# A two-layer diffusion backbone: bias among the first unit's matmuls, two modulation pieces moved, two more PSUM banks, new early order

## The reference

```
x += 0.5*g * swiglu(modulate(rms_norm(x)))        # half step, d_ff 2816
x +=     g * mixer(modulate(rms_norm(x))) @ w_out # attention A | windowed attention B | bidirectional SSD
x += 0.5*g * swiglu(modulate(rms_norm(x)))
```

## Time and profile before

| | us |
|---|---|
| median of 3 runs | 1890.67 |
| runs | 1890.6 to 1891.48 |
| the profiled execution | 1888.78 |
| its span, first to last instruction | 1887.1 |
| PE busy | 1811.9 (96%) |
| DVE busy | 1423.3 (75%) |
| ACT busy | 752.0 (40%) |
| mean granted TensorE clock | 0.968 of 2.4 GHz |

### The profile page before, as it was taken

How to read it: one execution, slowest core, us unless ns; L and a number is a source line. 1 busy time by engine, 2 the same in 40 slices (tenths; PEclk the granted TensorE clock), 3 DMA queues, 4 the chain that set the end, 5 groups by cost and what they waited for, 6 DMA issues and landing times.

```text
span 1887.1 us, 26111 instructions
## 1 busy us (share of the span) xinstructions
PE 1811.9 (96%) x9314; PEld 1496.1 (79%) x9314; DVE 1423.3 (75%) x2351; ACT 752.0 (40%) x1147; POOL 51.6 (3%) x101
## 2 busy tenths in 40 slices
PE   8999999997999899899999999999999799899999
PEld 5788888886776577688888888888888578589999
DVE  5887877788877767887777678777786888756665
ACT  4322222246656656222222372222224654754342
POOL 1000000000000000000000000000000000000000
PEclk8899999998998899899999999999999899979999
DMA  8444444422312033534444423444440332134543
GB/s 352 179 151 183 147 159 168 182 80 93 119 45 90 1 134 116 197 133 178 155 156 161 151 75 148 159 168 162 156 156 29 114 111 88 48 112 178 180 178 110
DMA packets 37585, 259.47 MB, mean 137 GB/s; under 512 B 4369, under 2 KB 5841, under 8 KB 7441
## 3 DMA queue, kind: packets, MB, share of 16 engines
q1 hardware_dynamic: 26066, 182.32, 26.5%
q0 software_dynamic: 11456, 76.32, 11.0%
HBM read 252.60 MB, written 5.24 MB: 137 GB/s over the span
## 4 chain that ended last, share of the span: by engine, by line
PE 84%; DVE 6%; ACT 6%; issue 3%; DMA 1%; POOL 0%; ACTq 0%; DVEq 0%; POOLq 0%
PE ps L1514 25%; PE ps L1515 25%; PE ps L1516 25%; PE ps L1622 1%; DVE mod_prod L951 1%; ACT w_hi L546 1%; ACT n_t L598 1%; PE ps L1830 1%; DMA scale_w<-scale_in 1%; PE ps L1772 1%; PE ps L1891 1%; PE ps L1795 1%; DVE x_res L1056 1%; PE ps L1805 1%; PE ps L1645 1%
## 5 line engine op out<-in xcount | busy, mean ns | idle before, releaser
L1514 PE MATMUL ps<-h_hi,w_hi 128*128 128x512 f32 (+1 forms) x1840 | 680.3, 370 | 26.3 <-DVE w_lo L933 10.4
L1515 PE MATMUL ps<-h_lo,w_hi 128*128 128x512 f32 (+1 forms) x1840 | 673.7, 366 | 0.0
L1516 PE MATMUL ps<-h_hi,w_lo 128*128 128x512 f32 (+1 forms) x1840 | 672.9, 366 | 0.0
L1514 PEld LDWEIGHTS ps<-h_hi,w_hi 128*128 128x128 f32 x1840 | 350.5, 190 | 90.7 <-issue 22.9
L1516 PEld LDWEIGHTS ps<-h_hi,w_lo 128*128 128x128 f32 x1840 | 350.2, 190 | 57.4
L1515 PEld LDWEIGHTS ps<-h_lo,w_hi 128*128 128x128 f32 x1840 | 350.6, 191 | 56.6 <-issue 1.2
L928 DVE TENSOR_TENSOR w_lo<-raw,w_hi 128x2048 fp32r<-128x2048 f32 x132 | 301.9, 2287 | 82.3 <-ACT w_hi L546 82.2
L1056 DVE SCALAR_TENSOR_TENSOR x_res<-ps,abg,x_res 128x256 f32<-128x256 f32 x584 | 248.4, 477 | 151.2 <-PE ps L1516 150.2
L546 ACT ACTIVATE w_hi<-raw 128x2048 fp32r<-128x2048 f32 x132 | 252.2, 1911 | 268.0 <-PE ps L1516 268.0
L951 DVE CUSTOM_DVE_ANT_0 mod_prod<-mod_raw,cb 128x1024 f32<-128x1024 f32 x256 | 301.5, 1218 | 2.6 <-ACT cb L738 2.5
L1514 PE MATMUL ps<-a_hi,w_hi 128*128 128x512 f32 (+1 forms) x640 | 235.5, 368 | 16.1 <-DVE x_res L1056 12.5
(11 more groups left out here) (231 smaller groups left out, 1594.9 us busy)
## 6 DMA issues: line engine op xcount, KB each, us to landing
raw<-ffn_in SPq DMA_DIRECT2D x132, 1024.0 KB, 4.8
mod_raw<-mod_in POOLq DMA_DIRECT2D x68, 1024.0 KB, 5.0
raw<-proj_in SPq DMA_DIRECT2D x20, 1024.0 KB, 4.9
raw<-out_w_in SPq DMA_DIRECT2D x8, 1024.0 KB, 4.7
x_spill<-x_res SPq DMA_DIRECT2D x2, 2048.0 KB, 7.2
x_res<-x_spill SPq DMA_DIRECT2D x2, 2048.0 KB, 7.9
scale_w<-scale_in POOLq DMA_DIRECT2D x4, 512.0 KB, 13.1
x_res<-x_in SPq DMA_DIRECT2D x2, 1024.0 KB, 11.3
```

What stands on the lines that cost most here:

```text
L1514: pe.matmul(dst, w_hi[:, slot, wsl], hi, start=first, stop=False)
L1515: pe.matmul(dst, w_hi[:, slot, wsl], lo, start=False, stop=False)
L1516: return pe.matmul(dst, w_lo[:, slot, wsl], hi, start=False, stop=last)
```

## The change

1. **Bias.** `unit_bias` is gone. `first_unit` waits until bank 4 is free and puts each bias matmul right behind the main matmul that uses the same weights. With 512 tokens the mean still stands after k = 2, with 256 after k = 5.
2. **Pieces.** Pieces 14 and 15 are done in f=0, no longer at the start of f=1. In turns 1 to 4 of f=0 there are three pieces for each two turns; the later ones follow one place on.
3. **Banks.** Tiles 3 and 4 go to banks 5 and 6. Tiles 0 to 4 wait for no evacuation, 5 and 6 for tiles 0 and 1.
4. **Order.** Norm tiles (`n`), `first_scaled` (`e`), the layer's vectors (`la`), the derive steps (`dv`) and the split of unit 2 (`S.-1`), which stood before the mixer's list, are steps of it. The decay rows have five parts instead of four (old part 1 is cut in two). The early half of both lists is in another order; from the attention on they are nearly the same.

```diff
-        MOD_PRE = {0: (2, 2), 1: (14, 2)}
+        MOD_PRE = {0: (2, 2)}
-        STRETCH = {0: [(1, PAIRS - 1, 4)], 1: [(1, PAIRS - 1, 16)], ...
-        LAST_PIECE = {0: 13}
+        STRETCH = {0: [(1, 5, 4), (5, PAIRS - 1, 10)], 1: [(1, PAIRS - 1, 16)], ...
+        LAST_PIECE = {0: 15}
         def tile_bank(g):
-            return g if g < 3 else (g + 1) % 2
+            return g if g < 3 else g + 2 if g < 5 else (g + 1) % 2
 WEAVE, layer 0, its beginning
-  "cv.0 E.0 E.1 S.0 T0.0 T.2 E.2 R.0 R.1 R.2 E.3 cv.1 T.3 T.4 cv.2 S.1 R.3 E.4 E.5 si.0 cv.3 S.2 si.1 si.2 si.3 cv.4 cv.5 T.5 T.6 T.7
+  "T0.0 la.0 T.2 S.-1 n.0 n.1 Ta.4 Tb.4 n.2 n.3 n.4 n.5 n.6 n.7 Ta.5 Tb.5 Ta.6 E.0 E.1 e.0 n.8 cv.0 E.2 S.0 R.0 R.1
+   R.2 R.3 si.0 cv.1 cv.2 E.3 Tb.6 S.1 R.4 cv.3 Ta.7 E.4 Tb.7 Ta.8 Tb.8 dv.0 E.5 si.1 S.2 cv.4 E.6 E.7 S.3
 WEAVE, layer 1, its beginning
-  "cv.0 T0.0 cv.1 T.2 E.0 E.1 E.2 R.0 R.1 T.3 T.4 T.5 S.0 E.3 si.0 T.6 T.7 E.4 R.2 S.1 cv.2 cv.3 R.3 S.2
+  "la.0 T0.0 T.2 Ta.4 n.0 Tb.4 Ta.5 Tb.5 n.1 Ta.6 n.2 Tb.6 n.3 n.4 Ta.7 Tb.7 Ta.8 n.5 n.6 n.7 e.0 n.8 S.-1 E.0 cv.0
+   cv.1 E.1 E.2 R.0 R.1 R.2 S.0 E.3 R.3 R.4 cv.2 S.1 cv.3 si.0 si.1 Tb.8 E.4 E.5 S.2
 POOL, load_stretches, and likewise VectorE
+                    if (f, lo) == (0, 1):
+                        with pool.Fori(0, 2) as t:
+                            for q in range(3):
+                                load_piece(3 * t + (q0 + q))
 VectorE, feed-forward
-                if f == 1:
-                    mod_pieces(q0, cnt // 2)
...
                 derive(n, "g")
+                if f == 1:
+                    dve.wait_ge(cb_ready, 6)
+                def turn(i, tiles):
+                    middle = 1 + len(tiles) // 2
+                    down(i - 1, base + 3 * i + 1, tiles=tiles[:2], gate_split=(2, f, i))
+                    split(0, f, i + 1)
+                    for tile in tiles[2:middle]:
+                        mod_tile(*tile)
+                    dve.wait_ge(unit_done, base + 3 * i + 2)
+                    product(f, i, nt, a_hi, a_lo)
+                    split(1, f, i + 1)
+                    for tile in tiles[middle:]:
+                        mod_tile(*tile)
 TensorE
+            def first_unit(n, turn, nt, hi, lo, evac, tile=None):
                 split_ready(0, turn)
+                pe.wait_ge(shift_done, 2 * n)
+                pe.wait_ge(*evac)
                 for k in range(KT):
                     pe.wait_ge(u_lo_s, 8 * (n - 1) + k + 1)
                     for m in range(2):
+                        dst, to, wsl = ps[:, m, 0:nt], ps[:, BIAS_AT, 4 * m:4 * m + 4], slice(...)
+                        pe.matmul(dst, w_hi[:, 0, wsl], hi[:, k, 0:nt], start=(k == 0), stop=False)
+                        pe.matmul(to, w_hi[:, 0, wsl], shift_r[:, k, :], start=(k == 0 and m == 0), stop=False, ...)
+                        pe.matmul(dst, w_hi[:, 0, wsl], lo[:, k, 0:nt], start=False, stop=False)
+                        x = pe.matmul(to, w_lo[:, 0, wsl], shift_r[:, k, :], start=False, stop=(k == KT - 1), ...)
+                        last = pe.matmul(dst, w_lo[:, 0, wsl], hi[:, k, 0:nt], start=False, stop=(k == KT - 1))
...
-                    if k == 2:
+                    if k == (2 if nt == T else 5):
                         mean(n, nt)
-                    elif k == 5:
-                        unit_bias(n, 0)
 TensorE, project
-                    pe.wait_ge(pj_evac, NT * layer + (g - 2 if g < 5 else g - 1))
+                    if g > 4:
+                        pe.wait_ge(pj_evac, NT * layer + (g - 4 if g < 7 else g - 1))
```

More of the change, by code:

```diff
@@ L693, in mixer @@
                     if kind == "E":
-                        if j >= 2:
+                        if j < 2:
+                            first_evacuation(layer, j)
+                        else:
                             evacuate(layer, j)
+                    elif kind == "n" and j < KT:
+                        norm_tile(3 * layer + 1, j, T, base)
                     elif kind == "S":
@@ L699, in mixer @@
                         decay_rows(layer, j)
-                        if layer == 0 and j == 3:
+                        if layer == 0 and j == 4:
                             act.wait_ge(masks_in_s, 16)
@@ L743, in first_evacuation @@
                 act.wait_ge(pads, layer + 1)
-                for j in range(2):
-                    act.wait_ge(scaled_s, 2 * n - 1 + j)
-                    for s in range(2):
-                        x = act.activation(xpad[:, j, s, 2:2 + LAT], ps[:, j, s * LAT:(s + 1) * LAT], ACT.Identity, bias=bias[:, j, s:s + 1])
-                    x.then_inc(pj_evac, 1)
+                act.wait_ge(scaled_s, 2 * n - 1 + j)
+                for s in range(2):
+                    x = act.activation(xpad[:, j, s, 2:2 + LAT], ps[:, j, s * LAT:(s + 1) * LAT], ACT.Identity, bias=bias[:, j, s:s + 1])
+                x.then_inc(pj_evac, 1)
             def evacuate(layer, g):
@@ L1020, in first_scaled, with norm_tile @@
                     tt(ps[:, m, 0:nt], ps[:, m, 0:nt], n_rstd[:, 0:nt], ALU.mult).then_inc(scaled_s, 1)
-            def norm_rest(n, nt, after={}):
-                def remainder(d):
-                    dve.wait_ge(h_hi_s, 8 * n + d + 1)
-                    tt(h_lo[:, d, 0:nt], n_t[:, d % 2, 0:nt], h_hi[:, d, 0:nt], ALU.subtract).then_inc(h_lo_s, 1)
-                dve.wait_ge(acc_done, 7 * n + 7)
-                dve.wait_ge(rstd_done, 2 * n + 2)
-                for d in range(KT):
+            def norm_tile(n, d, nt):
+                if d == 0:
+                    dve.wait_ge(acc_done, 7 * n + 7)
+                    dve.wait_ge(rstd_done, 2 * n + 2)
+                if d < KT:
                     if d >= 2:
@@ L1034, in norm_rest @@
                     tt(n_t[:, d % 2, 0:nt], x_res[:, d, 0:nt], n_rstd[:, 0:nt], ALU.mult).then_inc(t_done, 1)
-                    if d >= 1:
-                        remainder(d - 1)
+                if d >= 1:
+                    dve.wait_ge(h_hi_s, 8 * n + d)
+                    tt(h_lo[:, d - 1, 0:nt], n_t[:, (d - 1) % 2, 0:nt], h_hi[:, d - 1, 0:nt], ALU.subtract).then_inc(h_lo_s, 1)
+            def norm_rest(n, nt, after={}):
+                for d in range(KT + 1):
+                    norm_tile(n, d, nt)
                     if d in after:
                         after[d]()
-                remainder(KT - 1)
             def product(f, i, nt, hi, lo):
@@ L1087, in ffn_phase, with down @@
                 derive(n, "g")
-                def down(i, units, add_n=None, piece=None, gate_split=None):
+                if f == 1:
+                    dve.wait_ge(cb_ready, 6)
+                def down(i, units, add_n=None, tiles=(), gate_split=None):
                     for d in range(KT):
@@ L1099, in down @@
                             split(*gate_split)
-                        if piece is not None and d in (3, 7):
-                            mod_tile(piece, d // 4)
+                        if tiles and d in (3, 7):
+                            mod_tile(*tiles[d // 4])
                         if add_n is not None and d >= 2:
@@ L1105, in down @@
                             scaled_low(add_n[0], d - 1, add_n[1], h_hi, h_lo)
-                def turn(i, piece):
-                    down(i - 1, base + 3 * i + 1, piece=piece, gate_split=(2, f, i))
+                def turn(i, tiles):
+                    middle = 1 + len(tiles) // 2
+                    down(i - 1, base + 3 * i + 1, tiles=tiles[:2], gate_split=(2, f, i))
                     split(0, f, i + 1)
-                    if piece is not None:
-                        mod_tile(piece, 2)
+                    for tile in tiles[2:middle]:
+                        mod_tile(*tile)
                     dve.wait_ge(unit_done, base + 3 * i + 2)
@@ L1114, in turn, with tiles_of @@
                     split(1, f, i + 1)
-                    if piece is not None:
-                        mod_tile(piece, 3)
+                    for tile in tiles[middle:]:
+                        mod_tile(*tile)
+                def tiles_of(piece):
+                    return [] if piece is None else [(piece, j) for j in range(4)]
                 def last_turn(piece):
@@ L1133, in ffn_phase @@
                 for lo, hi, q in STRETCH[f]:
-                    with dve.Fori(lo, hi) as i:
-                        turn(i, None if q is None else i + (q - lo))
+                    if (f, lo) == (0, 1):
+                        with dve.Fori(0, 2) as t:
+                            a, b, c = (tiles_of(3 * t + (q + k)) for k in range(3))
+                            turn(2 * t + 1, a + b[:2])
+                            turn(2 * t + 2, b[2:] + c)
+                    else:
+                        with dve.Fori(lo, hi) as i:
+                            turn(i, tiles_of(None if q is None else i + (q - lo)))
                 last_turn(LAST_PIECE.get(f))
@@ L1171, in mixer @@
                         split_next(layer, j + 3)
+                    elif kind == "n":
```

(25 more changed lines are left out.)

93 lines of the change are left out of this document (45 added, 48 removed), and 69 rows, old and new, of the table WEAVE.

## The result

The changed kernel takes 1875.2 us (median of 4 runs, 1872.16 to 1877.52), the one before 1890.63 (1888.71 to 1891.48). The ratio is 0.9921, with a 95% interval of 0.9909 to 0.9934: 0.8% faster. Forecast were 1871 us and a range of 1858 to 1881. The profiled execution took 1876.09 us with a span of 1874.4, so 12.7 us of the 1887.1 us span of before are gone, where the forecast had 19.3.

A forecast was written before the change was run, and what follows sets the result against it. TensorE, busy 96% of the span, was taken as the bound. Terms summed to -19.3 us from the profiled 1888.78, giving 1869.5, plus 1.9 for the median: 1871 us; range 1858 to 1881.

The forecast's parts named there:

- Start of f=1, -15.4: Start of f=1: without the two pieces it falls to the length of f=2, -15.4 us (12 to 17 gained).
- f=0, +0.3: Turns 1 to 4 of f=0: the added products fit VectorE's idle time, +0.3 us (0 to +4).
- Bias at 0.11 us each: First units: interleaved bias matmuls cost 0.11 us each as before, nothing saved (bounds 0.03 to 0.25 each).
- The rival in which the loads reach further ahead: Bias matmuls: weight loads reach further ahead, bias at 0.03 us, whole kernel 1864 us; chance 0.06.
- Clock won, mean later, a new wait of 1.6 us: First units of f=1, f=2: 1.7 us of clock won, mean 1.33 later, new wait 1.6 for the split; -0.2 and -0.1.
- First mixer, -1.8: First mixer: tile 7 waits for S.1, 3.5 us won, 1.7 lost again to the clock: -1.8 us (-12 to +3).
- Second mixer, -0.6 (-12 to +4): Second mixer: split S.0 comes slightly earlier, mean +1.33 against -1.9 for steps taken out: -0.6 us (-12 to +4).
- f=3, -1.5 (-5 to +3): Last phase, 256 tokens: half the half-clock stretch of the bias block returns to full clock, -1.5 us (-5 to +3).

The follow-up runs named there:

- the two moved steps: Changed kernel with two second-layer steps moved, rotation c.6 to ahead of hy.2 and derive steps dv.0 to behind b.0: 1872.96 us, ratio to before 0.9913.

## Why the prediction was right, and where it was off

- *Start of f=1, -15.4:* measured 380.62 to 365.50 us from mean to mean, -15.1, and alone -15.4 (365.20). The reading was right: two f phases of one shape differ by what only one of them does. This term is the result. One sentence of its working is wrong and changes no term: a granted clock of 0.68 between 1.2 and 2.4 GHz means two thirds of the 21 us at 1.2 GHz, not one third; the 6.7 us lost are right.
- *f=0, +0.3:* +0.7 us for everything up to the first mixer. VectorE's idle times went, as worked out from the earlier trace rows, and TensorE did not wait.
- *Bias at 0.11 us each:* 0.12. The rival in which the loads reach further ahead is out. The Trainium skill (TensorE: Matmul & The Clock Gate, the step on LDWEIGHTS) lets loads be pulled ahead of running matmuls; this trace shows one load ahead, as the earlier trace rows did.
- *Clock won, mean later, a new wait of 1.6 us:* f=1 and f=2 got a first unit of 15.54 us at clock 1.00 (16.64 and 16.99 before), and from there to the next gate tile 1.2 and 1.7 us more, of which 1.49 us are the new stop. Forecast -0.2 and -0.1, measured +0.3 each (f=1 against the pieces alone). The waiter was right, the last cause was not: the first silu behind its table load ends 0.56 us after the split that I named. It hangs on the same chain of norm tiles, so the size held, and the mean behind k = 1 moved the stop by 0.9 us.
- *First mixer, -1.8:* -2.9. S.1 was forecast to end at 468.4 and ended at 468.95, in a mixer that starts 0.6 us later, so its chain was read right. TensorE was ready at 463.25 and not at 461.8, so the stop is 5.76 us, not 6.6. Counted from the mixer's first matmul, tile 7 begins 3.5 us earlier (55.96 to 52.43 us), as forecast, and 1.7 us are lost again from there to matmul 2640, early in the attention (120.5 to 122.2), as forecast. The further 1.0 us lies in the 120 matmuls behind it (37.7 to 36.7), with 17 instead of 24 us at half clock. That its clock would stay was assumed without a word, and that this came out in favour is luck: in four kernels (bias alone, the old order of layer 0, and the two with the mean behind k = 1) the mixer is 6 to 13 us longer by the clock of its attention.
- *Second mixer, -0.6 (-12 to +4):* +9.6, outside its bounds. This is the step that failed. The early half came out in its sum (-1.2), but not in its parts: the stops are 7.14 and 4.72 us where about 7 us and nothing further was said, and tile 5, held by S.0, begins 46.15 us behind the mixer's first matmul, 0.95 later than before instead of 0.6 earlier; the first unit, without half clock behind its bias, made up for it (16.99 to 15.54 us). The late half was taken as unchanged since its steps are nearly the same. In the new order `c.6` stands behind `hm.15`, TensorE is ready for the scores 1.8 us before VectorE has the rotation, and 27 us of half clock follow instead of 7. The late half is 10.7 us longer, and the two moved steps give back 8.6. In the five other profiles with this list and this stop the late half takes 108.6 to 113.8 us, in the four with the two steps moved 104.8 to 105.6. How a stop of 1.8 us brings that much half clock is not shown.
- *f=3, -1.5 (-5 to +3):* -5.2, just past its bound, by the clock: 20 us at half clock went. Part of what that gives was lost again to waits for the norm chain (0.92, 0.43 and 2.69 us). The reason given, that the block of the bias is gone, is not borne out: with the bias interleaved alone, and with the old order of layer 1, these units have 17 us at half clock and take 27.1 us, and three kernels with the block take 24.4. This gain is luck as far as the prediction goes.

In sum the stages gave -12.6 us instead of -19.3. Of the 6.7 us missing, 10.2 are the second mixer and 3.7 came back in f=3, both by clock; the rest is spread. The forecast time is only 4 us off, since the profiled execution of before was 1.9 us below its median and that of after is 0.9 above; that too is luck.

What stays open: the two banks were not tried alone (orders and banks together, with the bias in a block, are 1.1 us below the pieces alone, within the intervals), and which moment or work decides whether TensorE's clock falls in the attention and at f=3. A late half of 103 to 106 us always had a slow start of f=3 (clock 0.63 to 0.79, eight kernels). A late half of over 110 us had a fast one (1.00) wherever the mean of f=3 stood behind k = 5 (four profiles). The length of the stop ahead of it does not decide it, since 1.34 us was followed by half clock and 1.85 us was not.

## What to carry to other kernels

Compare phases of the same shape before anything else: the phase that does one thing more shows the price of moving it, and this one reading gave the whole result. Test the parts of a combined change alone: here the moved pieces give all of it, the interleaved bias alone costs 13 us, and with the new order of the first mixer beside it that loss is gone (the old one brings it back). And give every stage in which TensorE works on short or waited-for matmuls a term for its clock, of both signs: a shift of about 1 us upstream moved the first mixer by 6 us (mean behind k = 1) and by 11 us (bias alone, against the pieces alone), and no wait in it grew by as much.

## What the runs showed of the hardware

- Two profiles of the same program show the same two stages to 0.1 us and 0.01 of clock (113.85 us at 0.88, then 22.20 us at 1.00). Other executions of it have another mean clock (0.978 for 0.975), and kernels with the same list in that stage show other half-clock times (14 to 27 us).
- A short matmul with its own weights costs 0.12 us among 512-column matmuls and 0.11 in a block. Among them it left the clock at 2.4 GHz in all four first units of 512 tokens, in each kernel that has it so (15.5 to 15.9 us); at 256 tokens the first unit had half clock in six of ten profiles. A block of 32 went with half clock in all five first units of the kernel before, and in four of five in the kernel with moved pieces: not in the second mixer's, which took 15.41 us instead of 16.99.
- Half of the added half-clock time comes near the difference between stages: +20.5 us went with +11.4 (bias alone against pieces alone, first mixer), +27.3 with +13.4 (old order of layer 0), +20.5 with +10.7 (late half of the second mixer).
